# Splitting each weight panel into its high and low part in one piece instead of two halves

## The reference, cut to what matters

```python
h = rms_norm(x, w) * (1.0 + scale) + shift
y = mixer(h)                     # y = h @ w_in, ..., @ w_out
x = x + gate * y
x = x + gate2 * (jnp.square(jax.nn.relu(h2 @ w1)) @ w2)        # layers 0 and 1
x = x + gate2 * norm((jax.nn.silu(h2 @ w_g) * (h2 @ w_u)) @ w_d)   # layers 2 and 3
```

## Time and profile before

| | |
|---|---|
| median of the three runs | 2435.79 us |
| the profiled execution | 2436.39 us |
| its span from the first to the last instruction | 2434.6 us |
| TensorE busy | 2067.3 us (85%) |
| VectorE busy | 1540.6 us (63%) |
| ScalarE busy | 888.2 us (36%) |
| `w_low` (L365), VectorE | 408 instructions, 472.8 us busy |
| `w_high` (L357), ScalarE | 408 instructions, 401.7 us busy |

### The profile page before, as it was taken

One profiled execution on the slowest core, in us unless ns is written; L12 is line 12 of the kernel. 1 busy time (PEld: TensorE's weight loads), 2 busy tenths in 40 slices (PEclk: granted clock), 3 DMA queues, 4 the chain that ended last, 5 costly groups with the idle time before them and its releaser, 6 DMA issues. The chain is left out here.

```text
span 2434.6 us, 39903 instructions
## 1 busy us (share of the span) xinstructions
PE 2067.3 (85%) x16738; PEld 1840.4 (76%) x16738; DVE 1540.6 (63%) x2391; ACT 888.2 (36%) x1308; POOL 140.3 (6%) x231
## 2 busy tenths in 40 slices
PE   0898678799999679669997999799789979978997
PEld 0686466588888467548886899688679978867997
DVE  7865326699777556745654677679466656845544
ACT  2335224322222222142224444355444434544443
POOL 0000000001100001010120000000000000000000
PEclk9999778899999879879998999899899988979999
DMA  7441002255544344300001377533147743313552
GB/s 302 155 142 69 1 1 104 94 180 192 201 169 152 120 156 173 138 1 3 3 3 53 139 274 278 192 122 126 66 141 282 276 150 120 126 52 113 180 187 86
DMA packets 59020, 323.91 MB, mean 133 GB/s; under 512 B 6272, under 2 KB 7424, under 8 KB 32512
## 3 DMA queue, kind: packets, MB, share of 16 engines
q1 hardware_dynamic: 32960, 227.91, 26.2%
q0 software_dynamic: 25344, 92.29, 10.6%
q10 hardware_dynamic: 576, 1.70, 0.2%
HBM read 320.83 MB, written 1.05 MB: 132 GB/s over the span
## 5 line engine op out<-in xcount | busy, mean ns | idle before, releaser
L365 DVE TENSOR_TENSOR w_low<-raw,w_high 128x1024 fp32r<-128x1024 f32 (+1 forms) x408 | 472.8, 1201 | 263.0 <-ACT w_high L357 262.7
L357 ACT ACTIVATE w_high<-raw 128x1024 fp32r<-128x1024 f32 (+1 forms) x408 | 401.7, 1034 | 431.4 <-PE banks L395 385.8
L502 DVE SCALAR_TENSOR_TENSOR mod_rows<-mod_rows,silu_condition 128x1024 f32<-128x1024 f32 x176 | 212.4, 1221 | 46.2 <-DMA mod_rows<-rows_dram 44.5
L393 PE MATMUL banks<-ffn_a_l,w_high 128*128 128x256 f32 x704 | 199.8, 284 | 1.9 <-DVE ffn_hidden L864 1.9
L394 PE MATMUL banks<-ffn_a_h,w_high 128*128 128x256 f32 x704 | 199.3, 283 | 0.0
L395 PE MATMUL banks<-ffn_a_h,w_low 128*128 128x256 f32 x704 | 199.2, 283 | 0.0
L393 PE MATMUL banks<-mlp_a_l,w_high 128*128 128x512 f32 (+1 forms) x512 | 176.5, 345 | 11.9 <-DVE mlp_a_l L635 7.7
L488 POOL DMA_DIRECT2D mod_rows<-rows_dram x176 | 93.1, 529 | 1521.3 <-DVE mod_rows L502 1365.6
L394 PE MATMUL banks<-mlp_a_h,w_high 128*128 128x512 f32 (+1 forms) x512 | 175.2, 342 | 0.0
L395 PE MATMUL banks<-mlp_a_h,w_low 128*128 128x512 f32 (+1 forms) x512 | 174.9, 342 | 0.0
L393 PE MATMUL banks<-mlp_hidden_l,w_high 128*128 128x512 f32 (+1 forms) x512 | 173.1, 338 | 1.3 <-DVE mlp_hidden_l L872 1.3
(11 more groups left out here) (582 smaller groups left out, 4924.5 us busy)
## 6 DMA issues: line engine op xcount, KB each, us to landing
raw<-panels_dram SPq DMA_DIRECT2D x204, 1024.0 KB, 4.8
mod_rows<-rows_dram POOLq DMA_DIRECT2D x176, 512.0 KB, 5.1
mod_0a_rows<-rows_dram SPq DMA_DIRECT2D x4, 2048.0 KB, 24.9
x_features<-x_features_dram SPq DMA_DIRECT2D x1, 2048.0 KB, 25.1
constants<-small_dram SPq DMA_DIRECT2D x1, 1660.5 KB, 16.3
silu_condition<-conditions_dram ACTq DMA_DIRECT2D x3, 512.0 KB, 6.0
out_dram<-x_features SPq DMA_DIRECT2D x1, 1024.0 KB, 4.8
constants<-small_dram SPq DMA_DIRECT2D x1, 736.5 KB, 5.7
```

The source lines that it names most:

```text
L357: self.nc.scalar.activation(self.wh[:, m % 2, cols], self.raw[:, slot, cols], ACT.Copy).then_inc(self.w_high, 1)
L365: self.nc.vector.tensor_tensor(self.wl[:, m % 2, cols], self.raw[:, slot, cols], self.wh[:, m % 2, cols].bitcast(F32), ALU.subtract).then_ ...
L393: self.nc.tensor.matmul(out, sh(k), ml(k), start=(opens and k == 0), stop=False)
L502: nc.vector.scalar_tensor_tensor(row if v == nv - 1 else self.scratch[:], row, 1.0, self.cond[v][:], ALU.mult, ALU.mult, accum_out=mod[:, ...
```

## The change

Each panel is split by one instruction on each of the two engines in place of two, which took a half of the columns each. The counts of the semaphores and everything that waits for them follow (one per panel in place of two). Nothing else is changed: panels, buffers, products and the order of all other instructions stay.

```diff
@@ split_act
-        for h in range(2):
-            cols = slice(h * width // 2, (h + 1) * width // 2)
-            self.nc.scalar.activation(self.wh[:, m % 2, cols], self.raw[:, slot, cols],
-                                      ACT.Copy).then_inc(self.w_high, 1)
+        self.nc.scalar.activation(self.wh[:, m % 2, 0:width], self.raw[:, slot, 0:width],
+                                  ACT.Copy).then_inc(self.w_high, 1)
@@ split_dve
-        for h in range(2):
-            cols = slice(h * width // 2, (h + 1) * width // 2)
-            dve.wait_ge(self.w_high, self.in_loop(lambda x: 2 * x + h + 1, m, q))
-            self.nc.vector.tensor_tensor(self.wl[:, m % 2, cols], self.raw[:, slot, cols],
-                                         self.wh[:, m % 2, cols].bitcast(F32),
-                                         ALU.subtract).then_inc(self.w_split, 1)
+        dve.wait_ge(self.w_high, self.in_loop(lambda x: x + 1, m, q))
+        self.nc.vector.tensor_tensor(self.wl[:, m % 2, 0:width], self.raw[:, slot, 0:width],
+                                     self.wh[:, m % 2, 0:width].bitcast(F32),
+                                     ALU.subtract).then_inc(self.w_split, 1)
@@ wait_split
-        pe.wait_ge(self.w_split, self.in_loop(lambda x: 2 * x + 2, m, q))
+        pe.wait_ge(self.w_split, self.in_loop(lambda x: x + 1, m, q))
@@ stream
-                    sp.wait_ge(self.w_split, q * (2 * RAW) + 2 * (s - RAW + 1))
+                    sp.wait_ge(self.w_split, q * RAW + (s - RAW + 1))
...
-                sp.wait_ge(self.w_split, 2 * (n - RAW + 1))
+                sp.wait_ge(self.w_split, n - RAW + 1)
```

## The result

| | before | after |
|---|---|---|
| median (runs, lowest to highest) | 2436.09 us (4, 2434.53 to 2437.86) | 2464.22 us (4, 2459.79 to 2465.62) |
| ratio | 1 | **1.0112**, interval 1.0095 to 1.0130 (+23 to +32 us) |
| profiled execution; span | 2436.39; 2434.6 | 2460.01; 2458.2 |

The change makes the kernel slower. Forecast were 2458 us (2448 to 2467) and +22.3. The two profiled executions lie 23.6 us apart, the medians 28.

A forecast was written before the change was run, and what follows sets the result against it. Bound taken: the relay TensorE, ScalarE's copy, VectorE's subtraction, and who waits behind it, less what is spare. Terms 9.1 + 5.9 + 2.6 + 4.7 = +22.3 us gave 2458 us against 2435.79; range 2451 to 2465, wider 2448 to 2467.

The forecast's parts named there:

- One instruction for two: Every panel's split: where VectorE waits for ScalarE, it now waits for all 2048 columns, +0.80 us a panel.
- Feed-forward of layers 1 and 2: Steps with a row product before `hidden`: TensorE's up panel starts 0.65 us later, 14 times (9.1) and 9 times (5.9).
- Layer 3's steps: Layer 3's feed-forward: no row products, so the 0.80 us delay fits in 1.30 us spare and costs nothing.
- Layer 0: First five feed-forward steps of layer 0: TensorE waits for the later addition, 0.67 + 3 x 0.42 + 0.65 = 2.6 us.
- Mixers and ends: Mixers and last feed-forward step: delayed splits on the path cost 7.0 us, less savings of 1.3 and 1.0; together +4.7.
- The single relays: Mixers and ends: splits on the path where VectorE waits for ScalarE cost 0.80 us each, 8 x 0.80 = 6.4.
- The stream: SyncE's refills: a buffer may be refilled up to 0.8 us later, but panels land long before use; nothing.
- Fewer instructions win: Rival, whole kernel: saved instruction overhead reaches the path and waiting costs nothing; -2.3 us (2433.5) or -13 (2423); 4%.
- The loops hide it: Rival, feed-forward loops: they absorb the delay and only mixers and ends pay, +4.7 us, 2440.5; 7%.
- It costs more than the waits: Rival, feed-forward steps: TensorE's pauses lower its clock or a second wait forms behind `hidden`; 2481 us and above; 6%.

The follow-up runs named there:

- the first series: The changed kernel (one split instruction per engine and panel) timed against the kernel before: 2464.22 us against 2436.09, ratio 1.0112.
- the second: The changed kernel timed again without edit, with more rounds and a second profile, against the kernel before: 2460.67 us, ratio 1.0097.

## Why the prediction was right

*One instruction for two, +0.80 per panel.* Right: 0.79 in the step of layer 2 (4.16 against 3.37). The small saving where VectorE alone is late was also there: from VectorE's split of panel 107 to that of 112, five panels later, 41.95 us before (1645.22 to 1687.17) and 41.62 after (1661.75 to 1703.37), 0.33 less or 0.066 for each panel against the forecast 0.064.

*Feed-forward of layers 1 and 2, 23 x 0.65 = 15.0.* Right in mechanism, number and place; the 23 steps grew by 9.53 + 5.99 = 15.5 us. Where the distance was 0.29 or 0.30 before, a step grew by 0.64 to 0.66, as forecast. The rest is that I took this room for all steps. In layer 1 one step's matmul was recorded 0.07 behind `hidden` already before (1460.11 after 1460.04), so it had nothing to spare, and it grew by 0.79; three more had 0.23 or 0.24 and grew by 0.77, 0.78 and 0.70. In layer 2 the first two had 0.24 and grew by 0.76 and 0.70. (With 0.15 needed these should be 0.70 to 0.71; why three of them paid nearly all of it is open.) By the times, the loops alone cost 17.0 (11 to 22).

*Layer 3's steps, nothing.* Right; at panel 175 and at panel 203 the two traces are the same 22.80 us apart, to 0.01 us.

*Layer 0, 2.6.* Measured 2.45 from panel 21 to 31, in steps of 0.67, 0.44, 0.36, 0.38 and 0.60.

*Mixers and ends, +4.7.* The single relays came as forecast: in layer 2's mixer the copy of panel 107 is 0.79 further behind than that of panel 106, in layer 3's that of panel 160 0.84 further than that of 159. The panel of the earlier trace rows is taken by TensorE 0.06 us after the wide split (1614.98 after 1614.92). The row product behind the split of the earlier trace rows began at 882.62; now the split begins at 881.53 and the row product follows it at once, at 883.74.

Here I overlooked a term: the last feed-forward step of a layer waits for the low part of `hidden`, which is late by 0.80 as well. I charged it for layer 1 only; layers 2 and 3 pay it too (`ffn_hidden_l`, twice, new). The copies' starts fall back by 0.80 there in layer 2, and the end of the kernel by 0.78 behind the last copy in layer 3: 1.6 us that stand in no term. By the times, everything outside the two loops costs 8.4 (6 to 12). Like for like, the prediction has 2.6 + 4.7 - 0.8 = 6.5 there (the 0.8 of layer 1's last step lies in its loop), and with layer 3's overlooked 0.8 it is 7.3.

That the 23.6 of the traces lie so near the forecast 22.3 is in part luck. From the copy of panel 66 to that of 68, at the end of layer 1's mixer, the trace before takes 28.69 us at a granted clock of 0.82 and the one after 26.06 at 0.93. The kernel with the row product moved has the same code as the changed one there, and takes 28.69 at 0.82. So 2.6 us of clock stand against the cost; without them the traces give 26.2, about 4 above the forecast: 0.5 in the steps, 1.6 in the two last steps, and the rest, some 2, in the stretches between, the mixers above all, where single traces differ by more than that.

*The stream, nothing.* Right: ScalarE's waits for a landed panel are two, 28.1 us together before and 28.0 after.

*The rivals.* "Fewer instructions win" fell: VectorE got 12.0 us less busy and ScalarE 18.3, against 12 and 19 by the overheads that the Trainium skill gives (Perfetto Trace Analysis, Optimizing Scalar/DVE Operations), an estimate; on engines that stand waiting it bought nothing. That section offers grouping for a saturated engine only, and for engines that are not saturated but make others wait it says that breaking instructions up may help; the prediction's "by this rule alone" left this out, and the runs agree with it. "The loops hide it" fell by the 23 new waits. "It costs more than the waits" fell too: the clock stayed 1.00 in the steps of layer 2 with all their new gaps (window above), over the span it is 0.920 after and 0.919 before, and the steps grew by no more than the delay. (One argument against this rival was misread: the window of the earlier trace rows begins at 1809.00, just behind the wait of 0.9 us for the first `hidden`, and holds none.)

What stays open: medians and traces differ by 0 to 5 us (28.1 and 23.6 in the first series, 24.3 and 24.3 in the second), and I can't say which relays of the mixers make up what they cost.

## What to carry to other kernels

Two instructions that hand data from one engine to another in halves are not overhead to be merged: the second engine works on the first half while the first makes the second, and one wide instruction on either side ends that at the price of half the producer's time. Before you merge, read whether the consumer waits for the producer or is itself late; then follow the list behind the consumer to the next engine that waits, and subtract what that one has to spare. A loop pays the rest once in every turn.

## What the runs showed of the hardware that I had not expected

The clock that TensorE is granted in a mixer differs between executions of the same code by more than most terms here. From the copy of panel 151 to that of panel 175 the kernel before and the one that is wide only in the loops run the same instructions; the one took 245.10 us at a granted clock of 0.86, the other 239.16 at 0.90 (stretch, its us, busy us of TensorE's matmuls and weight loads, VectorE, ScalarE and GpSimd, granted clock, DMA share, GB/s). The changed kernel took 245.11 at 0.87.

```profile
1999.80:2244.90 245.10, 204.55 (x1407) 190.03 (x1408) 157.99 (x302) 115.42 (x210) 0.00 (x0) 0.86 0.28 100
```
```profile
2017.14:2256.30 239.16, 197.54 (x1407) 182.52 (x1408) 157.95 (x302) 115.45 (x210) 0.00 (x0) 0.90 0.29 103
```

The end of layer 1's mixer, panels 66 to 68, is a second such place, before and in the changed kernel:

```profile
1352.03:1380.72 28.69, 23.91 (x124) 18.73 (x122) 16.85 (x34) 13.31 (x25) 0.00 (x0) 0.82 0.28 103
```
```profile
1356.84:1382.90 26.06, 21.09 (x123) 17.44 (x122) 16.71 (x32) 13.13 (x23) 0.00 (x0) 0.93 0.33 117
```

It has two lengths and nothing between, whatever the split: in the twelve profiles of this case it takes 28.6 to 28.8 us at 0.82 eight times, and 26.0 to 26.1 at 0.93 four times. Panels 151 to 157 do the same, 48.5 to 49.0 us at 0.78 seven times and 45.2 to 45.6 at 0.87 to 0.88 five times.

So a term of the mixers must not be read from one pair of traces over a long stretch: the kernel that is wide only in the loops shows +11.4 us by its span and +17.0 by the medians, and the 5.9 us of the first stretch above make up that difference. In the stretches where TensorE hardly rests the traces repeat far better: nine steps of layer 2 grew by 6.05 and 6.06 us in the two profiles of the changed kernel, ten of layer 1 by 6.94 and 7.20.
